# The MLP down-projection of a two-block transformer: seven block products in place of eight, in passes of pairs

## The chip, the cores and the metric

The kernel runs on one core of a Trainium2 chip. The metric is the device time of one execution in microseconds; the numbers shown are medians of the runs.

## The reference

A sequence of 1,024 tokens of width 1,024 (float32) goes through two layers and then an attention block. In each layer x = x + g1 * mixer(modulate(rmsnorm(x))) and then x = x + g2 * mlp(modulate(rmsnorm(x))). The mixer of layer 0 is a pooling over windows, that of layer 1 a spatial gating unit; the shifts, scales and gates come from six vectors a layer, silu(c) @ ada_w + ada_b. The part that is changed is

```python
def sq_relu_mlp(h, w1, w2):
    return jnp.square(jax.nn.relu(h @ w1)) @ w2
```

with w1 of 1,024 x 4,096 and w2 of 4,096 x 1,024.

## The kernel before

Activations stand transposed, features on the 128 partitions and tokens along the free dimension in two halves of 512. A float32 product is made of three matmuls in a reduced float32 form: each operand is split into hi (ScalarE copies and so rounds it) and lo (VectorE subtracts hi from it), and `product` issues Whi.Xhi, Whi.Xlo and Wlo.Xhi (lines 2341 to 2343, a helper for most stages). X, of 8 rows (tiles of 128 features) by two halves, is resident except in the MLP, where its place is lent and it is reloaded from x_saved.

The hidden layer has 32 tiles of 128 features, in 16 pairs. `mlp` (line 599) drives all engines through one list of steps. The up-projection computes its first two pairs plainly (first_up, first_tile) and the other 14 in `fast`: each pair is a product of 2 x 2 blocks, done with 7 block products over sums of blocks (T1 to T4 on the token side, S1 to S4 on the weight side; the order is in PRODUCTS), each of 12 matmuls. VectorE joins the products, ScalarE takes relu and square, then hi; VectorE makes lo (`hidden_lo`), and SP stores hi and lo together in DRAM, 512 KB a tile and half.

The down-projection (`down`) goes over 16 chunks of one pair each. A chunk's weights, 1 MB, come through a ring of four stage slots and are split whole (L1223 on ScalarE, L1696 on VectorE); its hidden tiles come back already split into MB, issued on ScalarE's queue two chunks ahead. For each of 16 output tiles there are 2 products (6 matmuls) into one of four banks, and VectorE adds the bank, times the gate, to X (L2035). In layer 0 sixteen quarters of the ada vectors (1,2) to (1,5), 1 MB each with two VectorE instructions (L1671, L1674, L1677), are read between the chunks. In the last chunk the next norm has begun: `completed` squares each row, POOL adds the squares (L1077), TensorE sums them over partitions (L2373), and the first half's normed tiles are written before the second half's products end.

After layer 0 comes the value stage of the gating unit: `values` multiplies 8 token tiles by weights in four units (L2656 to L2658), 24 matmuls a tile and half, interleaved in SP's queue with the gather of the attention's position bias (L1018); `spatial` loads ws and bs and masks ws on POOL; `gates` follows. After layer 1 come the head projections.

```python
for c in range(CHUNKS):
    for a in late.get(c, ()):
        fetch(4)
        ada_ahead(*a)
    fetch(4)
    do["fetched_split"](T, None)
    used(w=1)
    do["down"](T, gate, l, c, then if c == CHUNKS - 1 else None)
```

## Time and profile before

| | |
|---|---|
| median of 3 runs | 2523.53 us (2520.54 to 2524.2) |
| span of the profiled execution, first to last instruction | 2519.7 us |
| its own time | not given apart from the runs; 3.8 us lie between its span and the median |
| TensorE, VectorE, ScalarE, POOL busy | 2460.9, 1636.2, 986.4, 273.9 us |
| down-projection, layers 0 and 1 | about 438 to 804 and 1419 to 1780 us |

Matmuls overlap, so their busy times add up to more than passes; their pace is read from one start to the next. The page also gives the granted clock of TensorE, as a share of 2.4 GHz; its two levels are 1.0 and 0.5, and values between them are means over a stretch.

### The profile page before, as it was taken

The numbers are of one execution on the slowest core, as the hardware profiler recorded it, in microseconds if no ns is written. First come the engines' busy times: TensorE is split into PE (matmuls) and PEld (weight loads), VectorE is DVE, ScalarE is ACT, GpSimd is POOL, SyncE is SP. The second block draws the span as 40 slices with busy tenths as digits, with TensorE's granted clock in tenths as the row PEclk, the third lists the DMA queues.
The fourth block names the chain that finished last, engine by engine and source line by source line (L and its number), as shares of the span: only waits on it lengthen the run. The fifth ranks groups of instructions, "written<-read, shape, count | busy, mean of one in ns | idle before, by whom it ended". The sixth has DMA issues, their size and how long they took to land.

```text
span 2519.7 us, 32563 instructions
## 1 busy us (share of the span) xinstructions
PE 2460.9 (98%) x11616; PEld 2003.8 (80%) x11616; DVE 1636.2 (65%) x2554; ACT 986.4 (39%) x1622; POOL 273.9 (11%) x279
## 2 busy tenths in 40 slices
PE   7999999999999999999999999999999999999998
PEld 2588888788887888888888888888888897886677
DVE  7798776777776343458667666666651226998873
ACT  2366565000003232237666300001431226887851
POOL 0200000000002000100000000000010002557731
PEclk9899999999999999999999999999999999999999
DMA  8726666855543610333544844431334472346621
GB/s 306 267 76 234 226 223 260 317 190 178 200 167 108 178 46 1 134 117 142 192 159 167 317 176 140 145 134 51 126 121 146 143 184 71 85 111 160 168 68 67
DMA packets 219076, 396.89 MB, mean 158 GB/s; under 512 B 59440, under 2 KB 136368, under 8 KB 218928
## 3 DMA queue, kind: packets, MB, share of 16 engines
q1 hardware_dynamic: 203696, 336.21, 40.3%
q10 hardware_dynamic: 15232, 58.72, 6.4%
q8 instruction: 91, 1.49, 0.2%
q14 instruction: 57, 0.47, 0.1%
HBM read 285.83 MB, written 115.08 MB: 159 GB/s over the span
## 4 chain that ended last, share of the span: by engine, by line
PE 87%; DVE 5%; issue 3%; POOL 3%; ACT 1%; DMA 0%; DVEq 0%; POOLq 0%; ACTq 0%; SPq 0%
PE banks L2341 23%; PE banks L2343 23%; PE banks L2342 23%; PE banks L2432 2%; PE banks L2871 2%; PE banks L2889 2%; PE banks L2656 1%; PE banks L2657 1%; PE banks L2658 1%; POOL probs L1139 1%; PE banks L2495 1%; DVE neg_max L2278 1%; PE banks L2373 1%; PE banks L2858 1%; PE banks L2859 1%
## 5 line engine op out<-in xcount | busy, mean ns | idle before, releaser
L2035 DVE SCALAR_TENSOR_TENSOR X<-banks,mod,X 128x512 f32<-128x512 f32 x512 | 380.8, 749 | 227.2 <-PE banks L2343 227.0
L2341 PE MATMUL banks<-Hhi,Whi 128*128 128x512 f32 x1248 | 493.3, 395 | 6.6 <-DVE Hlo L1861 2.9
L2342 PE MATMUL banks<-Hlo,Whi 128*128 128x512 f32 x1248 | 486.8, 390 | 0.0
L2343 PE MATMUL banks<-Hhi,Wlo 128*128 128x512 f32 x1248 | 486.8, 390 | 0.0
L2341 PE MATMUL banks<-MB,Whi 128*128 128x512 f32 x1024 | 401.5, 392 | 2.2 <-DVE X L2035 2.2
L2343 PE MATMUL banks<-MB,Wlo 128*128 128x512 f32 x1024 | 399.5, 390 | 0.0
L2342 PE MATMUL banks<-MB,Whi 128*128 128x512 f32 x1024 | 399.4, 390 | 0.0
L1223 ACT ACTIVATE Whi<-stage 128x2048 fp32r<-128x2048 f32 x59 | 112.9, 1913 | 615.3 <-PE banks L2343 577.2
L2341 PEld LDWEIGHTS banks<-Hhi,Whi 128*128 128x128 f32 x1248 | 235.1, 188 | 59.6 <-issue 8.3
L2342 PEld LDWEIGHTS banks<-Hlo,Whi 128*128 128x128 f32 x1248 | 235.1, 188 | 50.4 <-issue 2.4
L2343 PEld LDWEIGHTS banks<-Hhi,Wlo 128*128 128x128 f32 x1248 | 234.9, 188 | 49.4
L2341 PEld LDWEIGHTS banks<-MB,Whi 128*128 128x128 f32 x1024 | 192.9, 188 | 42.5 <-issue 3.0
L2343 PEld LDWEIGHTS banks<-MB,Wlo 128*128 128x128 f32 x1024 | 192.8, 188 | 40.4
L2342 PEld LDWEIGHTS banks<-MB,Whi 128*128 128x128 f32 x1024 | 192.9, 188 | 39.2
L1696 DVE TENSOR_TENSOR Wlo<-stage,Whi 128x1024 fp32r<-128x1024 f32 (+1 forms) x93 | 145.2, 1562 | 89.6 <-ACT Whi L1223 88.1
L1139 POOL TENSOR_SCALAR probs<-probs,rden 128x1024 f32<-128x1024 f32 (+2 forms) x128 | 118.3, 924 | 337.3 <-DVE rden L2284 327.6
L2289 DVE TENSOR_TENSOR PTl<-banks,PTh 128x512 fp32r<-128x512 f32 (+2 forms) x256 | 135.2, 566 | 6.6 <-ACT PTh L1609 5.5
L2871 PEld LDWEIGHTS banks<-const,probs 128*128 128x128 f32 x800 | 88.6, 140 | 56.8 <-DVE PTl L2289 22.6
L2341 PE MATMUL banks<-T,Whi 128*128 128x512 f32 x336 | 131.1, 390 | 0.0
L2871 PE MATMUL banks<-const,probs 128*128 128x128 f32 x800 | 116.5, 279 | 14.7 <-POOL probs L1139 9.2
L1609 ACT ACTIVATE PTh<-banks 128x512 fp32r<-128x512 f32 (+2 forms) x256 | 119.5, 504 | 29.1 <-PE banks L2871 26.2
L2343 PE MATMUL banks<-T,Wlo 128*128 128x512 f32 x336 | 130.8, 389 | 0.0
(247 smaller groups left out, 3773.2 us busy)
## 6 DMA issues: line engine op xcount, KB each, us to landing
stage<-w SPq DMA_DIRECT2D x64, 1024.0 KB, 6.1
hidden<-slot SPq DMA_DIRECT2D x112, 512.0 KB, 3.0
MB<-hidden ACTq DMA_DIRECT2D x56, 1024.0 KB, 5.6
stage<-ada_w SPq DMA_DIRECT2D x48, 1024.0 KB, 6.5
x_saved<-X SPq DMA_DIRECT2D x32, 512.0 KB, 3.1
stage<-w_in SPq DMA_DIRECT2D x13, 1024.0 KB, 6.2
X<-x_saved SPq DMA_DIRECT2D x24, 512.0 KB, 7.2
MB<-hidden SPq DMA_DIRECT2D x8, 1024.0 KB, 10.1
```

The costliest lines, as they stand in the source:

```text
L1139: nc.gpsimd.tensor_scalar(out=row, in0=row, scalar1=rden[:, u % 4:u % 4 + 1], scalar2=1.0, op0=ALU.mult, op1=ALU.mult).then_inc(probs_scal ...
L1223: nc.scalar.activation(Whi[:, T.n["w"] % 2, :], stage[:, s, :], ACT.Copy).then_inc(w_hi, 1)
L1609: nc.scalar.activation(probs_t(PTh, u, kind, first, m), TP[:, g, 0:m * P] .rearrange("p (k q) -> p k q", q=P), ACT.Copy).then_inc(th_done, 1)
L1696: ins = nc.vector.tensor_tensor(Wlo[:, w % 2, at], stage[:, u % STAGES, at], Whi[:, w % 2, at].bitcast(F32), ALU.subtract)
L2035: nc.vector.scalar_tensor_tensor(out=X[:, k, half(hf)], in0=Dn[:, i % D_BANKS, :], scalar=gate[:, k:k + 1], in1=X[:, k, half(hf)], op0=ALU ...
L2289: nc.vector.tensor_tensor(probs_t(PTl, u, kind, first, m), TP[:, g, 0:m * P].rearrange("p (k q) -> p k q", q=P), probs_t(PTh, u, kind, fir ...
L2341: nc.tensor.matmul(out_bank, whi, xhi, start=start, stop=False, skip_group_check=onto)
L2342: nc.tensor.matmul(out_bank, whi, xlo, start=False, stop=False, skip_group_check=onto)
L2343: return nc.tensor.matmul(out_bank, wlo, xhi, start=False, stop=stop, skip_group_check=onto)
L2432: ins = nc.tensor.matmul(row_bank(cc, h), c_act[:, 2 * q + k:2 * q + k + 1], stage[:, u % STAGES, k * D + h * H:k * D + (h + 1) * H], star ...
L2871: ins = nc.tensor.transpose(TP[:, g, k * P:(k + 1) * P], PE_[:, u % 2, a:a + P], con("ident"))
L2889: ins = nc.tensor.matmul(OB[:, g % 2, :], VT[:, e, k, :], x[:, g % 2, k, :], start=k == tiles[0] and x is PTh, stop=k == tiles[-1] and x i ...
```

## The change

The down-projection is done with 7 block products too. Its output has four groups (`o`) of two rows; the 16 pairs are summed in 18 passes (PASSES: group, first pair, pair behind the last), each over 2, 3 or 4 pairs, and at most 4 pairs' right operands (7 a pair, hi and lo) are on chip at a time. A pass has 7 products of 3 matmuls a pair in the banks A, B, C and D; after a product VectorE evicts a bank (D1, A1, B, C1, A2, C2, D2), partly to X and partly to a sum U of the group that is added to three blocks in the group's last pass.

The right operands (B11, B21, B22 and the sums T1 to T4) are stored raw, 256 KB each, and not split: the sums are made by VectorE in the fast units, by POOL for the last one. They come back through 8 tile buffers in the stage ring and are split in the passes by ScalarE and VectorE, each once a layer, in the steps that `right_steps` gives. The left operands of pass t+1 are summed by POOL (S1 to S4) and split by ScalarE and VectorE during pass t. Squares of finished groups are made in the following pass, and the norm begins after the last pass ("blocks"). The ada vectors (1,2), (1,3) and (1,4) are read in the value stage, and (1,5) in layer 1's fast units. The `rotation` load, semaphores and buffer places follow.

```diff
+OUTS = 4
+PASSES = ((0, 0, 2), (1, 0, 3), (2, 0, 4), (3, 0, 4), (0, 2, 6), (1, 3, 7), (2, 4, 8), (3, 4, 8), (0, 6, 10),
+          (1, 7, 11), (2, 8, 12), (3, 8, 12), (0, 10, 14), (1, 11, 14), (2, 12, 16), (0, 14, 16), (1, 14, 16),
+          (3, 12, 16))
...
+def first_needed(p):
+    return min(t for t in range(NPASS) if PASSES[t][1] <= p < PASSES[t][2])
+def made_during(p):
+    return -1 if p < 2 else p - 2 if p < 4 else max(t for t in range(NPASS) if PASSES[t][1] <= p - 4 < PASSES[t][2])
...
+def right_steps(t):
+    pairs = [p for p in range(CHUNKS) if made_during(p) == t]
+    steps = [[] for _ in range(len(SIDES) + 1)]
+    for n, p in enumerate(pairs):
+        for q in range(len(SIDES)):
+            steps[min(q + 2 * n, len(SIDES))].append((p, q))
+    return steps
+def raw_loads():
+    place = {}
+    for t in range(-1, NPASS):
+        for steps in right_steps(t):
+            for p, q in steps:
+                place[7 * p + q] = t
+    return [[n for n in range(RAW + 6, 7 * CHUNKS) if max(place[n - RAW], 0) == t] for t in range(NPASS)]
+def evictions(t):
+    o = PASSES[t][0]
+    names = ["D1"] + ([] if t == FIRST_PASS[o] else ["A1"]) + ["B"]
+    return names + (["U21", "U12", "U22"] if t == LAST_PASS[o] else []) + ["C1", "A2", "C2", "D2"]
...
-                stream.append(src_in(w1[l], p + 3) if p < PAIRS - 1 else src_w2(l, 0))
-            for c in range(CHUNKS - 1):
-                stream += [src_ada(*a) for a in late.get(c, ())] + [src_w2(l, c + 1)]
-            stream.append(after)
+                if p < PAIRS - 1:
+                    stream.append(src_in(w1[l], p + 3))
             fetched, consumed = 0, 0
...
+            for t in range(NPASS):
+                do["passes"](T, gate, l, t, base, then)
+                if t == NPASS - 2:
+                    do["fetch"](T, after, 0, 7 * (NPASS * l + NPASS - 1))
+            T.add(e=NPASS, u=1, w=1)
+            T.n["uc"], T.n["un"] = T.n["un"], T.n["u"]
...
-            for c in range(CHUNKS):
-                for a in late.get(c, ()):
-                    fetch(4)
-                    ada_ahead(*a)
-                fetch(4)
-                do["fetched_split"](T, None)
-                used(w=1)
-                T.n["uc"], T.n["un"] = T.n["un"], T.n["u"]
-                do["down"](T, gate, l, c, then if c == CHUNKS - 1 else None)
-                T.add(c=1, d=16)
-                if c in late and late[c][-1][2] == 3:
-                    mods(*late[c][-1][:2])
...
         do["values"](T, 0, range(1))
         T.add(a=1)
+        for q in range(4):
+            ada(1, 2, q)
         split(src_values(1, 0))
         do["values"](T, 0, range(1, 8))
         T.add(a=7)
+        for q in range(4):
+            ada(1, 3, q)
         split(src_values(1, 1))
         do["values"](T, 1, range(5))
         T.add(a=5)
+        for q in range(4):
+            ada(1, 4, q)
         split(src_in(sgu_in, 0))
         do["values"](T, 1, range(5, 8))
         T.add(a=3, c=4)
...
+            def load_raw(T, l, n):
+                p, q = n // len(SIDES), n % len(SIDES)
+                if n < 4:
+                    sync.wait_ge(unit_done, T("u", -1))
+                elif n < RAW:
+                    sync.wait_ge(unit_done, T("u"))
+                else:
+                    p0, q0 = (n - RAW) // len(SIDES), (n - RAW) % len(SIDES)
+                    sync.wait_ge(right_lo, split_by(l, p0, q0))
+                side_stored(l, p, q)
+                sync.dma_start(raw_tile(T, n), hidden[p, q]).then_inc(raw_in[n % RAW], 16)
...
+            def passes(T, gate, l, t, base, then):
+                g = PAIRS * (l + 1) - 1
+                if t + 2 < NPASS:
+                    load_pass(T, l, t + 2)
+                if t == 0:
+                    sync.wait_ge(m_square, 4 * g + 1)
+                    sync.wait_ge(joined, 5 * g + 3)
+                    reload_row(3)
+                    for n in range(4):
+                        store_sum(PAIRS - 1, g, n)
+                    sync.wait_ge(m_square, 4 * g + 2)
+                    sync.wait_ge(joined, 5 * g + 5)
+                    reload_row(6)
+                    for k, b, name in ((4, "22", "T2"), (5, "11", "T1"), (7, "21", "T4")):
+                        sync.wait_ge(b_stored[b], 16 * (g + 1))
+                        sync.wait_ge(t_stored[name], 16 * (g + 1))
+                        reload_row(k)
+                for n in LOADS[t]:
+                    load_raw(T, l, n)
...
+            def pass_sums(T, l, t, names):
+                n = NPASS * l + t
+                for name in names:
+                    if name == "S1":
+                        pool.wait_ge(pass_in[t % 2], 16 * (NPASS // 2 * l + t // 2 + 1))
+                        if t == 0:
+                            pool.wait_ge(unit_done, T("u"))
+                        else:
+                            pool.wait_ge(ps_lo, 7 * n)
+                        out, a, b, op = pass_columns(t, S_sum[:]), pass_block(T, t, 1, 0), pass_block(T, t, 1, 1), ALU.add
+                    elif name == "S3":
+                        pool.wait_ge(ps_sums, 4 * n + 1)
+                        out, a, b, op = pass_block(T, t, 1, 0), pass_block(T, t, 0, 0), pass_block(T, t, 1, 0), ALU.subtract
+                    elif name == "S2":
+                        pool.wait_ge(ps_lo, 7 * n + 1)
+                        out, a, b, op = pass_columns(t, S_sum[:]), pass_columns(t, S_sum[:]), pass_block(T, t, 0, 0), ALU.subtract
+                    else:
+                        pool.wait_ge(ps_sums, 4 * n + 3)
+                        pool.wait_ge(ps_lo, 7 * n + 3)
+                        out, a, b, op = pass_columns(t, S_sum[:]), pass_block(T, t, 0, 1), pass_columns(t, S_sum[:]), ALU.subtract
+                    nc.gpsimd.tensor_tensor(out, a, b, op).then_inc(ps_sums, 1)
+            def hidden_sum(g, n):
+                name = SUMS_MADE[n]
+                out, a, b = sum_tiles(name)
+                pool.wait_ge(m_square, 4 * g + 4)
+                reach(pool, t_stored[name], 16 * g)
+                if n > 0:
+                    pool.wait_ge(t_sums, 4 * g + n)
+                nc.gpsimd.tensor_tensor(out, a, b, ALU.subtract).then_inc(t_sums, 1)
+            def passes(T, gate, l, t, base, then):
+                g = PAIRS * (l + 1) - 1
+                if t + 1 < NPASS:
+                    pass_sums(T, l, t + 1, ("S1", "S3", "S2"))
+                    for n in range(4 if t == 0 else 0):
+                        hidden_sum(g, n)
+                    pass_sums(T, l, t + 1, ("S4",))
+                if then == 2:
+                    for n, o in enumerate(OUT_ORDER):
+                        if t == min(LAST_PASS[o] + 1, NPASS - 1):
+                            for i in range(4 * n, 4 * n + 4):
+                                add_squares(T, "blocks", i)
...
+            def passes(T, gate, l, t, base, then):
+                o = PASSES[t][0]
+                steps = right_steps(t)
+                if t == 0:
+                    for p, q in right_steps(-1)[len(SIDES)]:
+                        right_hi(T, l, p, q)
+                for q in range(len(SIDES)):
+                    act.wait_ge(pass_done, 7 * (NPASS * l + t) + q + 1)
+                    if q == 1 and t == FIRST_PASS[o]:
+                        nc.scalar.activation(UT[:, o, :], fast_bank("A", t), ACT.Copy).then_inc(u_begun, 1)
+                    if t + 1 < NPASS:
+                        pass_hi(T, l, t + 1, base, q)
+                    for p, r in steps[q]:
+                        right_hi(T, l, p, r)
+                    for n, done in enumerate(OUT_ORDER[:-1]):
+                        if t == LAST_PASS[done] + 1 and q < 4:
+                            block_square(T, l, 4 * n + q, then)
...
+            def evict(l, t, gate, name):
+                o, at = PASSES[t][0], {"D1": ("D", 0, "22"), "A1": ("A", 1, None), "B": ("B", 2, None), "C1": ("C", 3, "22"),
+                                       "A2": ("A", 4, "11"), "C2": ("C", 5, "21"), "D2": ("D", 6, "12")}
+                u = UT[:, o, :]
+                if name in at:
+                    bank, q, b = at[name]
+                    dve.wait_ge(pass_done, 7 * (NPASS * l + t) + q + 1)
+                    source = fast_bank(bank, t)
+                else:
+                    source, b = u, name[1:]
+                if b is None:
+                    if t == FIRST_PASS[o]:
+                        dve.wait_ge(u_begun, OUTS * l + t + 1)
+                    else:
+                        dve.wait_ge(evicted, evicted_by(l, t, name) - 1)
+                    nc.vector.tensor_tensor(u, source, u, ALU.add).then_inc(evicted, 1)
+                    return
+                x, k = out_tile(t, b)
+                if t == FIRST_PASS[o] and b in ("22", "11"):
+                    dve.wait_ge(x_filled[k], 16 * (l + 2))
+                dve.wait_ge(evicted, evicted_by(l, t, name) - 1)
+                nc.vector.scalar_tensor_tensor(out=x, in0=source, scalar=gate[:, k:k + 1], in1=x, op0=ALU.mult,
+                                               op1=ALU.add).then_inc(evicted, 1)
+            def passes(T, gate, l, t, base, then):
+                o = PASSES[t][0]
+                steps, last = right_steps(t), t == LAST_PASS[o]
+                if t == 0:
+                    for p, q in right_steps(-1)[len(SIDES)]:
+                        right_lower(T, l, p, q)
+                if t == NPASS - 3:
+                    make_gain(T, then)
+                for q, name in enumerate(("D1", "A1", "B", "C1", "A2", "C2", "D2")):
+                    if name in evictions(t):
+                        evict(l, t, gate, name)
+                    if q == 2 and last:
+                        for more in ("U21", "U12", "U22"):
+                            evict(l, t, gate, more)
+                    if t + 1 < NPASS:
+                        pass_lo(T, l, t + 1, base, q)
+                    for p, r in steps[q]:
+                        right_lower(T, l, p, r)
...
+            def passes(T, gate, l, t, base, then):
+                n = NPASS * l + t
+                o, p0, p1 = PASSES[t]
+                if t == 0:
+                    pe.wait_ge(joined, 5 * T.n["f"])
+                    pe.wait_ge(m_relu, 4 * T.n["f"] - 2)
+                for q, (_, side, bank, first) in enumerate(PRODUCTS):
+                    pe.wait_ge(ps_lo, 7 * n + q + 1)
+                    for p in range(p0, p1):
+                        if first_needed(p) == t:
+                            pe.wait_ge(right_lo, split_by(l, p, q))
+                    if t > 0:
+                        if q == 0 and t > 1:
+                            pe.wait_ge(evicted, evicted_by(l, t - 2, "D2"))
+                        if q == 1:
+                            pe.wait_ge(evicted, evicted_by(l, t - 1, "A2"))
+                        if q == 2:
+                            pe.wait_ge(evicted, evicted_by(l, t - 1, "B"))
+                        if q == 3:
+                            pe.wait_ge(evicted, evicted_by(l, t - 1, "C2"))
+                    if q == 4:
+                        if t == FIRST_PASS[o]:
+                            pe.wait_ge(u_begun, OUTS * l + t + 1)
+                        else:
+                            pe.wait_ge(evicted, evicted_by(l, t, "A1"))
+                    if q == 5:
+                        pe.wait_ge(evicted, evicted_by(l, t, "C1"))
+                    if q == 6:
+                        pe.wait_ge(evicted, evicted_by(l, t, "D1"))
+                    hi, lo = operand_at(base, q)
+                    for p in range(p0, p1):
+                        at = slice((p - p0) * P, (p - p0 + 1) * P)
+                        ins = product(fast_bank(bank, t), (hi[:, at], lo[:, at]), right_side(side, p % KH2),
+                                      first and p == p0, p == p1 - 1, not first)
+                    ins.then_inc(pass_done, 1)
...
```

## Rows read from the trace of the kernel before

**Rows 1.** the page, part 1: busy time, share of the span, instructions
```profile
PE 2460.9 (98%) x11616; PEld 2003.8 (80%) x11616; DVE 1636.2 (65%) x2554; ACT 986.4 (39%) x1622; POOL 273.9 (11%) x279
```
**Rows 2.** the page, part 5: the down-projection's additions and products, busy | idle before
```profile
L2035 DVE SCALAR_TENSOR_TENSOR X<-banks,mod,X 128x512 f32<-128x512 f32 x512 | 380.8, 749 | 227.2 <-PE banks L2343 227.0
...
L2341 PE MATMUL banks<-MB,Whi 128*128 128x512 f32 x1024 | 401.5, 392 | 2.2 <-DVE X L2035 2.2
```
**Rows 3.** timeline of PE, 759 to 773 us: first and last of 57 matmuls
```profile
759.62 0.39 PE L2341 MATMUL banks<-MB,Whi 128*128 128x512 f32 x1
...
772.32 0.39 PE L2343 MATMUL banks<-MB,Wlo 128*128 128x512 f32 x1
```
**Rows 4.** windows: PE, PEld, DVE, ACT, POOL busy; clock; DMA share, GB/s
```profile
550.00:600.00 50.00, 50.00 (x230) 41.66 (x229) 37.38 (x47) 5.75 (x3) 0.00 (x0) 1.00 0.56 190
850.00:900.00 50.00, 50.00 (x220) 40.89 (x218) 12.06 (x14) 10.60 (x14) 0.00 (x0) 1.00 0.32 90
```
**Rows 5.** lines by form, 200 to 400 us (the fast products)
```profile
L1932 DVE TENSOR_TENSOR Wlo<-stage,Whi 128x512 fp32r<-128x512 f32 x42 | 28.8, 686 | 6.6 <-ACT Whi L1389 6.6
...
L1389 ACT ACTIVATE Whi<-stage 128x512 fp32r<-128x512 f32 x42 | 26.1, 621 | 16.5 <-PE banks L2343 16.4
```
**Rows 6.** lines by form, DVE, 700 to 925 us
```profile
L1696 DVE TENSOR_TENSOR Wlo<-stage,Whi 128x2048 fp32r<-128x2048 f32 x5 | 11.5, 2291 | 3.9 <-ACT Whi L1223 3.9
...
L1677 DVE SCALAR_TENSOR_TENSOR acc<-stage,c_act,acc 128x1024 f32<-128x1024 f32 x3 | 3.9, 1285 | 0.1
```
**Rows 7.** timeline, 779 to 792 us: VectorE beside POOL
```profile
780.89 8.69 POOL L1077 TENSOR_TENSOR SUM<-SUM,SQ 128x512 f32<-128x512 f32 x5 [0.80 <-ACT SQ L1239]
...
783.42 2.17 DVE L1696 TENSOR_TENSOR Wlo<-stage,Whi 128x1024 fp32r<-128x1024 f32 x1
...
785.51 2.07 DVE L2035 SCALAR_TENSOR_TENSOR X<-banks,mod,X 128x512 f32<-128x512 f32 x3
```
**Rows 8.** timeline, 1813 to 1830 us: a POOL product and a VectorE sum
```profile
1819.73 1.29 POOL L1125 TENSOR_TENSOR COS<-QN,rope 128x512 f32<-128x512 f32 x1 [3.13 <-DVE QN L2217]
1820.29 1.28 DVE L2227 TENSOR_TENSOR RF<-COS,RT 128x512 f32<-128x512 f32 x1
```
**Rows 9.** lines by form, POOL, whole span
```profile
L1077 POOL TENSOR_TENSOR SUM<-SUM,SQ 128x512 f32<-128x512 f32 x38 | 52.2, 1377 | 87.7 <-ACT SQ L1239 86.0
...
L1132 POOL TENSOR_TENSOR ws<-ws,const 128x128 f32<-128x128 f32 x8 | 3.4, 461 | 37.2 <-DMA bs<-sgu_bs 37.2
```
**Rows 10.** the page, part 6: DMA issues, KB each, us to landing
```profile
stage<-w SPq DMA_DIRECT2D x64, 1024.0 KB, 6.1
hidden<-slot SPq DMA_DIRECT2D x112, 512.0 KB, 3.0
...
X<-x_saved SPq DMA_DIRECT2D x24, 512.0 KB, 7.2
```
**Rows 11.** timeline of PE, layer 0's last chunk to the first value matmul
```profile
774.25 0.49 PE L2341 MATMUL banks<-MB,Whi 128*128 128x512 f32 x1
...
810.64 0.77 PE L2656 MATMUL banks<-Whi,Hhi 128*128 128x512 f32 x1
```
**Rows 12.** timeline of PE, layer 1's end of the down-projection
```profile
1780.16 2.78 PE L2373 MATMUL banks<-g_sq,SQ 128*128 128x2 f32 x24
```
**Rows 13.** windows, PE alone: busy, granted clock, DMA share, GB/s
```profile
792.00:795.00 3.00, 3.00 (x13) 0.50 0.31 128
795.00:798.00 3.00, 3.00 (x9) 0.50 0.12 46
...
810.00:813.00 3.00, 3.00 (x12) 0.63 0.94 231
```
**Rows 14.** timeline of SP's queue, 800 to 925 us
```profile
817.76 11.14 SPq L1018 DMA_DIRECT2D position_bias<-rpb  x8
...
832.66 4.71 SPq L922 DMA_DIRECT2D bs<-sgu_bs  x1
```
**Rows 15.** timeline of POOL, 825 to 870 us
```profile
842.78 3.39 POOL L1132 TENSOR_TENSOR ws<-ws,const 128x128 f32<-128x128 f32 x8 [37.24 <-DMA bs<-sgu_bs]
```

More of the change, by code:

```diff
@@ L903, in fast @@
[L903 to L917 removed]
+                        store_sum(p - 1, g - 1, n)
```

576 lines of the change are left out of this document (325 added, 251 removed).

## The prediction

> **What bounds the kernel now.** I read the page first: TensorE is busy for 98% of the span [rows 1]. The costliest groups then say what it does: in the down-projection it waited 2.2 us in all for its 3,072 products, while VectorE's additions to X sat idle for 227 us waiting for products [rows 2]. So in this stage TensorE's issue rate sets the end. The "mean ns" of a matmul is no price, for matmuls overlap: in the timeline 56 start-to-start steps take 12.70 us, 0.2268 us each [rows 3]. Stretches of 50 us show the cover: VectorE 37.4 busy in the down stage, 12.1 in the value stage, TensorE 50.0 in both [rows 4].
>
> **What is removed.** A layer has 16 pairs of hidden tiles and 4 outputs of two rows each; 8 block products of 3 matmuls are 16 x 4 x 8 x 3 = 1,536 matmuls, 7 are 1,344. Two layers save 384 x 0.2268 = 87.1 us. Only new waits of TensorE can take it back, so each handover is walked below.
>
> **VectorE in a pass.** Three end-to-end additions take 2.07 us [rows 7]: one occupies 0.66 us, 0.09 less than its busy 0.75; the same allowance makes a subtraction in SBUF (0.687 busy [rows 5]) 0.60. A full pass (84 matmuls, 19.05 us) has seven evictions (5 x 0.66 + 2 x 0.60 = 4.5), seven left operands (4.2) and 0, 7 or 14 right ones (0, 4.2, 8.4): 8.7, 12.9 or 17.1 us. ScalarE has at most 21 copies of 0.62 [rows 5] = 13.1. POOL has four sums; one of 128x512 takes 1.29 us alone [rows 8] and 1.377 in the mean, 0.461 at 128 columns [rows 9]. They cost VectorE too: with POOL at work from 1819.73 for 1.29 us, a subtraction issued at 1820.29 took 1.28, that is 0.73 until POOL ended and then 0.55 of its own [rows 8]; the 128x1024 one took 2.17 [rows 7] where half of a 128x2048 one is 1.15 [rows 6]. Additions from a bank kept their pace beside the same POOL work [rows 7]. So I charge 2.5 to 4.5 us a pass (an eviction hides half of a blocked sum, a second subtraction nothing; bounds 0 and 5.2). The heaviest passes, 3, 7 and 11, come to 21.6 against 19.05. TensorE stands first at product 5, which needs eviction C1; in pass 4 I find C1 done 0.2 us before that, and the next pass (16.1) repays the lag. Price 0; if nothing is repaid, 3 x 2.6 a layer, 16 us. The Trainium skill, SBUF — State Buffer, Who interferes with whom, says that a VectorE instruction with two SBUF inputs and a GpSimd instruction that reads SBUF lock each other out whole; by that rule and by the row it is the same 5.2 us at most.
>
> **Start of the passes, the largest new wait.** In pass 0 SP's queue is: weights, row 3, the four right sums of the last unit, rows 6, 4, 5, 7, and only then the raw tiles from number 14 on. Tile 14 is pair 2, product 0. ScalarE wants it in step 0 of pass 0, ahead of the copy that begins U, for which product 4 waits. The sums are POOL's now, behind S1, S3 and S2 of pass 1. From the end of the last fast product: the last join and product 0's start at 2 (VectorE enters some 1.2 us late, with 12 right operands and 7 left ones in that unit); first left operand of pass 1 at 8, S2 9, four sums 4 x 1.3, 14.2; the store of T4 lands 3.0 later [rows 10], and row 7 waits for it, 17.3; tile 14 goes out at 17.7 behind 2 MB of rows, whose landing takes 7.2 [rows 10], so about 23; U at 24.5, product 4 until 25.8, C1 near 28. Products 5 and 6 end at 31 where an unhindered pass ends at 9.5. Pass 1 (14.3 us of products, some 17 of VectorE) then waits about 1, against lag already counted. I take 22 a layer, 44, less the 2.2 of before [rows 2]: +42. Low end, stores and rows landing in 2.6 to 3 and no queue: 12 a layer, +22. High end 27, +52.
>
> **End of the passes.** Passes 15 and 16 have 2 pairs (9.5 us of products), yet all evictions plus U21, U12 and U22 (3 x 0.66, in SBUF). In 15, C1 comes 8.2 after the start, product 5 could start at 6.8: 1.4. In 16 the operands of a 4-pair pass are split and S1, S3, S2 of it lie between: 3.4; in layer 0 POOL also adds squares, and ScalarE's squares wait for them: 5.3. Together 4.8 + 6.7, +12 (4 to 20).
>
> **Norms.** They no longer begin inside the last chunk. Layer 0 before: 774.25 to the first value matmul at 810.64 is 36.4 us [rows 11] for 96 matmuls (21.8): 14.6 lost. After: eviction, square, statistics, deviation, spread, first scaled and split tile, some 7.2, and 1.6 in the second half where VectorE's 1.3 a tile lags. -6. Layer 1 before: only 2.6 us of statistics stand between [rows 12]; after about 8, because both deviations stand ahead of the first tile: +7 with its statistics. Together +1 (-5 to +10).
>
> **Value stage, where 12 ada quarters now stand.** A quarter costs VectorE 2 x 1.28 [rows 6], 10 us for four, and a 1 MB load of 6.1 us [rows 10] in a ring of four. Before, SP was far ahead. Now the load of the unit behind four quarters waits for the first of them, and VectorE reaches that only after the statistics of all eight tokens. For unit (1,1), from the end of the first half: quarter 0 done at 5, load landed at 14 (the quarters' own loads go out behind eight bias DMAs, 11.1 us of SP [rows 14], and share the wires), ScalarE 1.9, VectorE 2.3 [rows 6]: 18.2; TensorE wants it after 4 tokens, 48 matmuls, 10.9: 7 to 9 us. Then ws and bs: behind the unit that waits for the first quarter of (1,4). bs issues for 4.7 us [rows 14] and its mask took 3.4 [rows 15]; they were there 50 us early, now the mask ends about 9 after the last value product. Together +17 (8 to 28). Layer 1's four quarters in the fast units cost 2.6 each in units with 3 us to spare: 0.
>
> **Clock.** After short stalls and small matmuls the granted clock was 0.50 at 792 to 795, and 0.63 at the restart at 810 [rows 13]; a restart costs 1 to 3 us of matmuls. Five new idle stretches of 5 us or more, some of whose restarts are bound by VectorE anyway: +6 (0 to 14).
>
> **Sum.** Against the profiled span, 2519.7: -87.1 + 42 + 12 + 1 + 17 + 6 = -9, 2510.6. The median, 2523.5, is 3.8 above that span (the profiled execution's own time isn't shown apart), so 2514.5, and I say 2515. About 0.2%, 5 us, is what a measurement here can tell from no change.
>
> **The rivals.**
> 1. *Fewer waits.* SP gets through its stores and the ring refills early: start +22, values +8, end +4, clock 0: 2523.5 - 87 + 35 = 2472; half way, 2485, is its typical result. For it: my walk takes each landing at its loaded value. Against: the order of the queue is fixed. Chance 0.26.
> 2. *The port.* POOL's sums block VectorE in every step, heavy passes aren't repaid: +16, and the start and end grow by 8: 2539, slower. It decides once C1 of pass 4 is over 2 us later than I find. For it: rows 8. Against: over passes 3 to 6 VectorE has 51.6 us and POOL 20.6 against 76.2. Chance 0.17.
> 3. *Late raw tiles.* A tile is loaded only once the one eight before is split. In passes 3, 7 and 11 I find 6.3 us between; a landing of 3.0 fits, one of 7.2 as for X's rows does not, and each heavy pass pays about 5: 6 x 5 = 30, 2545. Decides from a landing of 6.3. Chance 0.13.
> 4. *The clock.* It falls not at long gaps alone but in passes with many short waits, as around 792 to 798, where 6 us at half the clock lose 3 [rows 13]; ten such places give 2547. The Trainium skill, TensorE: Matmul & The Clock Gate, names such cycling through PSUM banks in "A second HAM failure mode"; the rows of before show it once a layer end at most. Chance 0.08.
> My forecast has 0.36, of which 0.21 is faster, 0.10 the same, 0.05 slower.
>
> **Chances and range.** Faster 0.21 + 0.26 = 0.47; same 0.10 + 0.03 from rivals 2 and 4 at their edges = 0.13; slower 0.40. The range, 2480 to 2550, reaches to typical rival 1 and past rivals 3 and 4; the likeliest case alone spans 2500 to 2530.
>
> **What would show it.** 2,688 matmuls in the passes at 0.227; TensorE idle some 15 us between products 3 and 5 of pass 0, released through ScalarE's U copy by the load of raw tile 14; full passes at 19.1 us; 1 to 5 us ahead of product 5 in passes 15 and 16; two waits of 7 to 9 us in the value stage, on Wlo and on the ws mask; 7 to 8 us at each norm. The forecast is wrong if tile 14 is there early, if VectorE subtractions beside POOL take 0.69, or if middle passes take over 20 us.

## The result, and the profile after

The changed kernel takes 2550.9 us (median of 4 runs, 2549.3 to 2556.6) against 2522.9 of the kernel before: a ratio of 1.0115, 95% interval 1.0100 to 1.0129. It is slower by 1.15%; I had forecast 2515, in a range of 2480 to 2550. The profiled span is 2547.4 us against 2519.7, 27.7 more.

The page first: its span, engines and costliest waits.

```profile
span 2547.4 us, 32726 instructions
PE 2411.7 (95%) x11232; PEld 1955.2 (77%) x11232; DVE 1694.2 (67%) x2714; ACT 1115.1 (44%) x1946; POOL 489.2 (19%) x431
...
L2665 PE MATMUL banks<-Hhi,Whi 128*128 128x512 f32 x1760 | 701.9, 399 | 66.7 <-ACT UT L1600 38.2
...
L2339 DVE SCALAR_TENSOR_TENSOR X<-banks,mod,X 128x512 f32<-128x512 f32 x180 | 134.5, 747 | 89.6 <-PE banks L2667 89.2
```

The 384 matmuls are gone, and TensorE is busy for 49 us less than in [rows 1], in a span that is 28 us longer. One wait stands out where [rows 2] had next to none: 38.2 us behind ScalarE's copy that begins U. The windows that answer to [rows 4] show a middle pass, and then the value stage:

```profile
550.00:600.00 50.00, 50.00 (x223) 41.40 (x222) 35.16 (x50) 18.25 (x32) 17.27 (x12) 1.00 0.38 122
850.00:900.00 50.00, 37.33 (x146) 29.87 (x147) 20.12 (x27) 11.48 (x14) 5.30 (x8) 0.87 0.46 150
```

In the middle passes TensorE is still full at clock 1.00, with VectorE at 35 of 50 us. In the window of the value stage it has lost 12.7 us to waits, and the granted clock is 0.87 in the mean. TensorE's timeline gives the waits themselves (start, duration, idle before and what ended it):

```profile
181.34 0.77 PE L2665 MATMUL banks<-Hhi,Whi 128*128 128x512 f32 x1 [3.05 <-DVE U L2239]
...
443.16 0.50 PE L2665 MATMUL banks<-T,Whi 128*128 128x512 f32 x1 [1.39 <-DVE full L2239]
...
467.92 0.76 PE L2665 MATMUL banks<-Hhi,Whi 128*128 128x512 f32 x1 [19.03 <-ACT UT L1600]
...
758.78 0.76 PE L2665 MATMUL banks<-Hhi,Whi 128*128 128x512 f32 x1 [3.50 <-DVE X L2339]
...
791.98 0.77 PE L2991 MATMUL banks<-Whi,Hhi 128*128 128x512 f32 x1
...
853.91 0.79 PE L2991 MATMUL banks<-Whi,Hhi 128*128 128x512 f32 x1 [5.75 <-DVE Wlo L1970]
898.49 3.78 PE L2955 MATMUL banks<-ws,ones 128*128 128x512 f32 x4 [8.76 <-POOL ws L1377]
...
1798.41 3.69 PE L2699 MATMUL banks<-g_sq,W_raw 128*128 128x2 f32 x32
1808.01 0.76 PE L2665 MATMUL banks<-Hhi,Whi 128*128 128x512 f32 x1 [3.65 <-DVE Hlo L2135]
```

These are the places that the prediction had walked: the handover, product 4 of pass 0, passes 15 and 16, the norms (791.98 answers to 810.64 in [rows 11], 1798.41 to 1780.16 in [rows 12]), Wlo and the mask in the value stage. The clock does not stay up in every pass. It is at 0.50 around the stall of pass 0 in both layers, and again for 10 us in pass 16 of layer 0, where two waits stand close together:

```profile
756.00:760.00 4.00, 1.22 (x3) 1.06 (x4) 2.59 (x4) 0.00 (x0) 1.89 (x2) 0.50 0.97 398
760.00:764.00 4.00, 4.00 (x10) 3.07 (x10) 2.04 (x3) 2.82 (x5) 3.71 (x4) 0.50 0.03 11
```

The windows of the gates stage, which comes next, show something that it had not walked (columns: TensorE busy and matmuls, granted clock, DMA share, GB/s):

```profile
920.00:925.00 5.00, 5.00 (x23) 1.00 0.75 238
925.00:930.00 5.00, 4.22 (x31) 0.83 0.02 5
930.00:935.00 5.00, 5.00 (x25) 0.50 0.00 0
935.00:940.00 5.00, 5.00 (x19) 0.50 0.00 0
940.00:945.00 5.00, 5.00 (x19) 0.80 0.00 0
```

TensorE counts as busy and does half the work: the clock is at the lower of its two levels (1.2 of 2.4 GHz) for some 14 us. The same happens at 966 and 1000, for 10 us each. The lines of this stage, 895 to 1045 us, tell what is new there:

```profile
L2666 PE MATMUL banks<-WSlo,Vhi 128*128 128x128 f32 x64 | 22.9, 358 | 0.0
L2688 PE MATMUL banks<-ones,X 128*128 128x1 f32 x48 | 5.8, 250 | 2.3 <-ACT X L1737 2.3
```

L2688 is the ada sums of vectors (1,2), (1,3) and (1,4): eight matmuls of 128x1 for each (two records a matmul), which the change moved from the down stage to stand between `gates(j)` and `mix(j)`. Mix's 128x128 matmuls behind them mean 358 ns; in the kernel before they were 275:

```profile
L2342 PE MATMUL banks<-WSlo,Vhi 128*128 128x128 f32 x64 | 17.6, 275 | 0.0
```

The ledger by stages, after minus before, from the start of each stage's first matmul, adds up to the 27.7 us:

| stage | before, us | after, us | difference |
|---|---|---|---|
| layer 0, first up to pass 0 (down) | 321.8 | 327.0 | +5.2 |
| layer 0, down with its norm | 372.7 | 348.8 | -23.9 |
| value stage, to the first gates matmul | 89.2 | 109.3 | +20.1 |
| gates and mix, to the first wait of the resplit | 112.5 | 138.5 | +26.0 |
| resplit, projection, norm | 94.3 | 94.3 | 0.0 |
| layer 1, first up to pass 0 | 312.5 | 320.9 | +8.4 |
| layer 1, down with its norm | 363.6 | 352.9 | -10.7 |
| the rest, with the opening | 853.0 | 855.6 | +2.6 |

Four sums of ada vectors stood in layer 0's down-projection before, 1.70 us each from their start to the next product's. So 6.8 of the 23.9 us that this stage gained are work that now stands elsewhere: three sums in the gates stage, and that of (1,5) in the fast units of layer 1, 1.7 of its +8.4.

### The profile page after: what moved, and what is told of

It is laid out like the page before. It is cut to its first block, busy times and chain, and to the rows that moved or that the text cites. A ratio compares the mean times of both kernels' runs of the same rounds, so it can differ in the third digit from the quotient of the medians.

```text
span 2547.4 us, 32726 instructions
## 1 busy us (share of the span) xinstructions
PE 2411.7 (95%) x11232; PEld 1955.2 (77%) x11232; DVE 1694.2 (67%) x2714; ACT 1115.1 (44%) x1946; POOL 489.2 (19%) x431
## 4 chain that ended last, share of the span: by engine, by line
PE 80%; issue 7%; DVE 5%; POOL 4%; ACT 2%; DMA 1%; SPq 0%; POOLq 0%; DVEq 0%; ACTq 0%
PE banks L2665 22%; PE banks L2667 21%; PE banks L2666 21%; PE banks L3206 2%; PE banks L3224 2%; PE banks L2743 2%; POOL probs L1384 1%; PE banks L3193 1%; PE banks L3194 1%; PE banks L2807 1%; DMA stage<-hidden 1%; PE banks L2699 1%; POOL X L1416 1%; PE banks L2688 1%; PE banks L3176 1%
## 5 line engine op out<-in xcount | busy, mean ns | idle before, releaser
L2665 PE MATMUL banks<-Hhi,Whi 128*128 128x512 f32 x1760 | 701.9, 399 | 66.7 <-ACT UT L1600 38.2
L2666 PE MATMUL banks<-Hlo,Whi 128*128 128x512 f32 x1760 | 692.4, 393 | 0.0
L2667 PE MATMUL banks<-Hhi,Wlo 128*128 128x512 f32 x1760 | 691.9, 393 | 0.0
L2665 PEld LDWEIGHTS banks<-Hhi,Whi 128*128 128x128 f32 x1760 | 335.3, 191 | 147.2 <-issue 66.3
L2666 PEld LDWEIGHTS banks<-Hlo,Whi 128*128 128x128 f32 x1760 | 335.5, 191 | 70.9 <-issue 2.7
L2665 PE MATMUL banks<-T,Whi 128*128 128x512 f32 x720 | 281.6, 391 | 2.9 <-DVE full L2239 2.9
L2667 PE MATMUL banks<-T,Wlo 128*128 128x512 f32 x720 | 280.2, 389 | 0.0
L2666 PE MATMUL banks<-T,Whi 128*128 128x512 f32 x720 | 280.2, 389 | 0.0
L2339 DVE SCALAR_TENSOR_TENSOR X<-banks,mod,X 128x512 f32<-128x512 f32 x180 | 134.5, 747 | 89.6 <-PE banks L2667 89.2
L2665 PEld LDWEIGHTS banks<-T,Whi 128*128 128x128 f32 x720 | 135.3, 188 | 31.5 <-DVE full L2239 3.8
L2667 PEld LDWEIGHTS banks<-T,Wlo 128*128 128x128 f32 x720 | 135.2, 188 | 28.4
L2666 PEld LDWEIGHTS banks<-T,Whi 128*128 128x128 f32 x720 | 135.4, 188 | 27.9
```

What stands on the lines that cost most here:

```text
L2339: nc.vector.scalar_tensor_tensor(out=x, in0=source, scalar=gate[:, k:k + 1], in1=x, op0=ALU.mult, op1=ALU.add).then_inc(evicted, 1)
L2665: nc.tensor.matmul(out_bank, whi, xhi, start=start, stop=False, skip_group_check=onto)
L2666: nc.tensor.matmul(out_bank, whi, xlo, start=False, stop=False, skip_group_check=onto)
L2667: return nc.tensor.matmul(out_bank, wlo, xhi, start=False, stop=stop, skip_group_check=onto)
```

## The experiments

All are edits of the changed kernel but one. "Ratio" is to the kernel before, with its 95% interval; value and gates are the two stages of the ledger, from each profiled run.

| run | median us | ratio | value, us | gates, us |
|---|---|---|---|---|
| before | 2522.9 | 1 | 89.2 | 112.5 |
| after | 2550.9 | 1.0115 (1.0100 to 1.0129) | 109.3 | 138.5 |
| e1_swap | 2536.3 | 1.0063 (1.0046 to 1.0080) | 107.7 | 122.0 |
| e1_early | 2544.7 | 1.0092 (1.0075 to 1.0109) | 124.8 | 114.2 |
| e2_raws | 2528.3 | 1.0030 (1.0020 to 1.0040) | | |
| e3_order | 2534.2 | 1.0054 (1.0036 to 1.0073) | 90.4 | 139.8 |
| e4_sums | 2532.5 | 1.0034 (1.0021 to 1.0047) | | |
| e5_all | 2495.3 | 0.9888 (0.9870 to 0.9906) | 90.6 | 123.7 |
| e6_nowait | 2547.1 | 1.0100 (1.0081 to 1.0118) | 109.9 | 133.9 |
| e7_noada | 2507.2 | 0.9942 (0.9924 to 0.9959) | 90.2 | 112.5 |
| e8_best | 2499.0 | 0.9904 (0.9887 to 0.9921) | 89.7 | 122.2 |
| e9_wide | 2539.9 | 1.0067 (1.0048 to 1.0087) | 107.9 | 128.4 |
| e10_before_sums | 2541.1 | 1.0074 (1.0056 to 1.0091) | 89.1 | 129.2 |
| e11_late | 2485.5 | 0.9863 (0.9845 to 0.9880) | 89.7 | 122.2 |

**The theory and its rivals.** Theory: the passes cost what I had worked out, and the loss beyond it is the moved ada sums, through the clock. Rivals: the stage is longer through waits; or the loss comes from the passes after all.

**e1_swap**, the sums behind mix, so that full-size matmuls follow them:

```
-            if j < 3:
-                mods(1, 2 + j)
             mix(j)
+            if j < 3:
+                mods(1, 2 + j)
```


> The three moved ada sums (1,2), (1,3), (1,4) are issued after mix(j) instead of before it, so that full-size gates matmuls follow them and not the 128x128 ones of mix. Theory A (the sums' wait and their 8 matmuls of 128x1, followed by the small matmuls of mix, let the granted clock fall to 0.50 for 10 to 12 us three times, some 15 to 18 us of the 26.0 us that the gates stage lost): the clock stays at or near 1.00 in the gates stage and the time falls by 12 to 20 us to 2531 to 2539. Rival B (the sums bring the clock down wherever they stand): the fall moves into the gates matmuls and the time stays within 4 us of 2551. Rival C (the stage is longer for other waits than the clock): the clock comes back, the stage keeps 15 or more of its 26 us.

14.6 us less by the medians; the gates stage is 16.5 shorter. Same instructions, other place. In the first of the three places the clock stayed up where it had fallen (columns from here on: TensorE, weight loads, VectorE, ScalarE and POOL busy, clock, DMA share, GB/s):

```profile
925.00:930.00 5.00, 5.00 (x47) 5.00 (x47) 4.24 (x7) 0.24 (x2) 0.00 (x0) 1.00 0.01 4
930.00:935.00 5.00, 5.00 (x30) 4.34 (x30) 4.84 (x8) 3.98 (x5) 0.00 (x0) 1.00 0.00 0
...
960.00:965.00 5.00, 5.00 (x17) 4.00 (x18) 4.91 (x7) 2.91 (x3) 0.00 (x0) 0.66 0.00 0
```

Mix's 128x128 matmuls mean 275 ns again, as in the kernel before. The clock still dips at the other two places, for 3.4 us each, to 0.66 in the window shown. Theory A holds, with some of rival B. The kernel before bears it out: its layer 0 has seven such sums in front of 128x512 products, between 261 and 774 us, and the clock is 1.00 after each of them.

**e1_early**, the sums ahead of the value stage's last wait:

```
         T.add(a=3, c=4)
+        for cc in (2, 3, 4):
+            mods(1, cc)
         do["spatial"](T)
```


> The three moved ada sums are all taken out of the gates stage: they are issued before the row sums of the spatial weights, at 889 to 898 us, where TensorE waits 8.8 us for POOL's mask, into three separate banks. Theory A: the gates stage returns to within 3 us of its 111.6 us of before, and the time falls by 20 to 26 us to 2525 to 2531; the value stage grows by 0 to 4 us. Rival B (the clock falls in mix for another cause than the sums): the gates stage keeps 10 us or more over 111.6 and the clock still falls there. Rival C (the gain is given back in the value stage, because the row sums now wait for the sums): the value stage grows by more than 5 us.

The gates stage returns to 114.2, as theory A says, with the clock at 1.00 from 924 us on, 3 us after its start. Yet 15.5 of the 24.4 us are given back in the value stage, rival C, by a step that I had overlooked: SP loads `ws` only when all modulations counted so far are done (`mod_done`), and now these three are among them, so POOL's mask comes later. TensorE waits 5.6 us ahead of the sums and 9.4 behind them, where it waited 8.8 once, and the clock is 0.50 from 896 to 924 us.

**e6_nowait**, the sums in their place without their wait for ScalarE:

```
-                reach(pe, a_free, T("a"))
+                if not (l == 1 and 1 < cc < 5):
+                    reach(pe, a_free, T("a"))
```


> The changed kernel with the moved sums where they are, ahead of mix, but without their wait for ScalarE's last activation of the gates (they write a bank that no activation reads), so the wait of 0.78 us and the gap of 1.16 us ahead of each go, or move behind the sums. Theory A1 (the 8 small matmuls and the small ones of mix alone lower the clock): the granted clock still falls to 0.50 after each of them, the time falls by 0 to 4 us. Theory A2 (the wait is needed for the fall): the clock stays near 1.00 and the time falls by 12 to 20 us, to 2531 to 2539.

A1. The gaps of 1.16 us are gone and the stage is 4.6 us shorter, while the clock falls as before, with TensorE never idle by the records:

```profile
925.00:930.00 5.00, 5.00 (x40) 4.81 (x38) 0.81 (x2) 0.60 (x1) 0.00 (x0) 0.93 0.36 126
930.00:935.00 5.00, 5.00 (x25) 5.00 (x25) 2.99 (x5) 0.00 (x0) 0.00 (x0) 0.50 0.00 0
935.00:940.00 5.00, 5.00 (x18) 4.33 (x18) 3.86 (x8) 3.09 (x5) 0.00 (x0) 0.55 0.00 0
```

**e10_before_sums**, the suspected cost alone, in the kernel before:

```
             def mix(T, j):
+                if j < 3:
+                    pe.wait_ge(bs_ready, KT)
+                    for n in range(KT):
+                        nc.tensor.matmul(B6[:, n:n + 1], ones[:], ones[:, 0:1], start=True, stop=True)
```


> The kernel before the change, with eight matmuls of 128x1 added ahead of mix's first wait for j = 0, 1 and 2 (their result is not read), and nothing else. Theory A (these small matmuls in front of mix's small ones are enough to lower the clock in this place): three stretches at 0.50, the time grows by 12 to 20 us over the kernel before, to 2534 to 2542. Rival B (it takes the later state of the changed kernel, its accumulations or waits on other engines): the time grows by the matmuls alone, 3 x 1.8 = 5 us, to 2524 to 2529.

0.74% slower than the kernel before, some 19 us, 16.7 of them in this stage: theory A's size. The added matmuls are busy for 5.5 us; the rest is the clock. It fell in two of the three places, not in all three as expected. These are the windows of TensorE alone, around the first fall and the place without one:

```profile
920.00:925.00 5.00, 5.00 (x36) 0.84 0.20 70
925.00:930.00 5.00, 5.00 (x25) 0.50 0.00 0
930.00:935.00 5.00, 5.00 (x18) 0.50 0.00 0
935.00:940.00 5.00, 5.00 (x19) 0.80 0.00 0
...
955.00:960.00 5.00, 5.00 (x41) 1.00 0.00 0
960.00:965.00 5.00, 5.00 (x39) 1.00 0.02 5
```

Twenty-four matmuls that cost 5.5 us by their durations thus cost about three times that, and nothing else of the change is needed for it.

**e9_wide**, 64 columns in place of one:

```
+                    for j in range(KT):
+                        ins = nc.tensor.matmul(B6[:, j * 64:(j + 1) * 64], ada_total(l, cc)[:, j * P:(j + 1) * P],
+                                               ones[:, 0:64], start=True, stop=True)
```


> The changed kernel with the moved sums where they are, ahead of mix, but each of their 24 matmuls made 64 columns wide in place of 1 (the result is read from every 64th column). Theory A (matmuls of one column leave TensorE nearly idle although the profile shows it busy, and this is what lowers the clock): with more columns the granted clock stays higher in the three stretches and the time falls by 5 to 20 us, to 2531 to 2546. Rival B (any pause of full-size matmuls before mix's matmuls of 128 columns lowers it, whatever the width of the sums): the clock falls to 0.50 as before, the time within 4 us of 2551 or some us above.

11 us less, 10 of them in the stage: wider matmuls that take no longer (5.9 us busy in place of 5.8). The clock stayed at 1.00 after the first and the third sums and fell after the second:

```profile
955.00:960.00 5.00, 4.58 (x33) 4.61 (x33) 0.79 (x2) 0.28 (x1) 0.00 (x0) 0.79 0.01 3
960.00:965.00 5.00, 5.00 (x25) 5.00 (x25) 2.78 (x5) 0.00 (x0) 0.00 (x0) 0.50 0.01 2
```

That is on theory A's side. With one column the clock fell in all 15 places of five profiled kernels (the changed one, e2_raws, e3_order, e4_sums, e6_nowait), and the ratio's interval here lies below that of the changed kernel. But e10_before_sums, with one column too, has two falls in three places, so how much of a single profile is chance stays open.

**e7_noada**, the three vectors left out:

```
-        for q in range(4):
-            ada(1, 2, q)
...
-            if j < 3:
-                mods(1, 2 + j)
```


> The three moved ada vectors (1,2), (1,3), (1,4) are left out: no loads, no accumulation, no sums; their part of the modulation is set to zero once at the start, so the output is not the reference's. Theory A (what the change lost outside the down passes is the move of these three vectors: 20.1 us in the value stage and 26.0 us in the gates stage): the time falls by 40 to 48 us to 2503 to 2511. Rival B (the value stage's wait for the mask is there without the vectors, since the mask's load stands behind the weights' loads on SP's queue and the shorter norm has moved it): 5 to 10 us of it stay, 2511 to 2520.

43.8 us less; both stages are back at 90.2 and 112.5, the one 1.0 us longer than in the kernel before, the other equal. So all that the two stages lost is these vectors' move. With everything else of the change in place the kernel is 0.58% faster than before, some 15 us. Part of that is work left out, which the kernel before still does: the three sums alone are 5.1 us of TensorE there. So the passes by themselves gain some 0.4% (an estimate from these two numbers).

**e3_order**, the value stage's order:

```
-        for q in range(4):
-            ada(1, 2, q)
         split(src_values(1, 0))
+        for q in range(4):
+            ada(1, 2, q)
         do["values"](T, 0, range(1, 8))
         T.add(a=7)
...
         split(src_values(1, 1))
+        do["ws_load"](T)
```


> In the value stage each split of value weights comes before the four ada quarters that the change put ahead of it, and the spatial weights and their bias are loaded right after the second split instead of after everything. Theory A (the 20.1 us that the stage lost are the wait of 6.1 us for the value weights behind the quarters at 847.8, the wait of 9.2 us for the mask at 889.3, and some 3 us of lower clock after them): both waits go and the time falls by 13 to 20 us to 2531 to 2538. Rival B (VectorE, or SP's eight issues for each position bias at 1.3 us each, sets these waits): at least one of the two waits stays over 3 us, gain 4 to 12 us.

Theory A: 16.7 us less. The value stage is 90.4, both waits are gone. The gates stage keeps its loss, so the two are separate.

**e2_raws**, raw tiles 14 to 20 first in SP's queue:

```
+                for n in LOADS[t] if t == 0 else ():
+                    if n < 3 * len(SIDES):
+                        load_raw(T, l, n)
                 if t + 2 < NPASS:
                     load_pass(T, l, t + 2)
```


> On SP's queue the seven raw right tiles of pair 2 are loaded at the start of pass 0, ahead of the weights of pass 2, the four stores of the last unit's sums and the five reloads of rows. Theory A (the stall of 19.4 us before product 4 of pass 0, in both layers, is the load of raw tile 14 queued behind those): the stall falls to 1 to 6 us, and the time falls by 2 x (12 to 17) = 24 to 34 us, to 2517 to 2527. Rival B (VectorE's splits or the transfers, which then crowd, bound passes 0 to 2): half of it returns as stalls in passes 1 and 2, gain 8 to 20 us. Rival C (the reloads of rows 4 to 7 or the stores, now later, are waited for): gain below 8 us, with waits for DMA X in passes 1 to 3.

22.6 us less, just short of theory A's 24. The long stall of layer 0 has become two shorter ones, of 2.3 and 5.9 us, ahead of products 4 and 5 (the expectations below call the latter product 6, counting from one). The second has VectorE in front of it, and VectorE's timeline of those us is this:

```profile
454.04 1.76 DVE L2268 TENSOR_TENSOR Hlo<-stage,Hhi 128x512 fp32r<-128x512 f32 x1
455.72 0.68 DVE L2337 TENSOR_TENSOR UT<-banks,UT 128x512 f32<-128x512 f32 x1
456.32 1.02 DVE L2260 TENSOR_TENSOR Wlo<-S_sum,Whi 128x384 fp32r<-128x384 f32 x1
457.26 1.74 DVE L2268 TENSOR_TENSOR T<-stage,T 128x512 fp32r<-128x512 f32 x1
458.93 0.74 DVE L2343 SCALAR_TENSOR_TENSOR X<-banks,mod,X 128x512 f32<-128x512 f32 x1
```

Subtractions in SBUF take 1.7 us beside POOL's sums and 0.68 without them; additions from a bank keep their pace. That is what [rows 7, 8] showed and rival 2 was about. Whether it costs time here, the next run asks. The Trainium skill, SBUF — State Buffer, Who interferes with whom, says that a VectorE instruction with two SBUF inputs contends with a GpSimd instruction that reads SBUF, and one with at most one SBUF input, outside some faster modes, does not. By that rule, the trace agrees: 1.76 and 1.74 us for the first kind, 0.68 and 0.74 for the second.

**e4_sums**, those four sums made by VectorE:

```
-                    for n in range(4 if t == 0 else 0):
-                        hidden_sum(g, n)
...
                         right_lower(T, l, p, q)
+                        if n == 1:
+                            for m in range(4):
+                                hidden_sum(PAIRS * (l + 1) - 1, m)
```


> The early raw loads of e2_raws, and the four sums of the last unit's hidden tiles made by VectorE between the raw tiles of pair 1 (446 to 450 us, where VectorE stood idle for 2.2 and 0.6 us) in place of POOL (453.7 to 460.1 us). Theory A (in e2_raws the stall of 6.1 us before product 6 of pass 0, in both layers, is the VectorE queue, whose subtractions took 1.49 to 1.76 us beside POOL's four sums in place of 0.68): the stall falls to 1 to 3 us, the rows of 1.49 to 1.76 us go, and the time falls by another 2 x (3 to 5) = 6 to 10 us against e2_raws, to 2518 to 2522. Rival B (VectorE's own count of instructions bounds this stretch, so four more of 0.68 us cost as much as they save): within 3 us of e2_raws at 2528. Rival C (the transfers bound it): within 3 us as well, with waits for DMA stage<-hidden.

A miss: the time is that of e2_raws within the intervals. The rows of 1.7 us are gone, but the sums ran at 451.1 to 454.4, in front of the splits and evictions that pass 0 waits for, and cost as much as they saved (rival B). They were not in the idle 2 us that I had aimed at.

**e5_all**, the four edits together:

> All together: early raw loads, last unit's sums on VectorE, the value stage's order of e3_order, the ada sums after mix as in e1_swap. If the causes are separate, the gains add: 22.6 (e2_raws) + 6 to 10 (e4_sums) + 16.7 (e3_order) + 14.6 (e1_swap) = 60 to 64 us from 2550.9, that is 2487 to 2491, faster than the kernel before by 1.2 to 1.4%. Rival (they overlap, a wait that is taken away uncovers another): 40 to 55 us, 2496 to 2511.

55.7 us less than the changed kernel, between the full sum and the rival's upper end; the shortfall of 4 to 8 us is about the gain that e4_sums had not shown. **e8_best** puts the sums into the idle time:

```
+                        if n == 0:
+                            for m in range(4):
+                                hidden_sum(PAIRS * (l + 1) - 1, m)
                         right_lower(T, l, p, q)
-                        if n == 1:
```


> As e5_all, but VectorE makes the last unit's four sums ahead of the last two raw tiles of pair 1, in its idle 2 us at 446.9 to 449.1, where e4_sums and e5_all had them at 451.1 to 454.4 us, in front of the eviction and the splits that pass 0 waits for. Theory A (VectorE's queue from 449 to 460 us is what products 4 and 6 of pass 0 wait for; the place of the sums cost what their cheaper rows saved): the stall of 6.3 to 6.6 us before product 6 falls to 2 to 4 us in both layers and the time falls by 4 to 8 us to 2487 to 2491. Rival B (the transfers of the raw tiles bound it): within 2 us of 2495.

Another miss, no difference to e5_all that the intervals show. The stall at product 5 did fall from 6.6 to 3.6 us in layer 0, but waits of 1.0 and 2.2 us came up in pass 1: between 440 and 520 us TensorE lost 11.5 us in e5_all and 11.7 here. This points to the sum of VectorE's work as what bounds passes 0 and 1, and not to one instruction's place.

**e11_late**, the first unit's sums behind the third join:

```
                 join(g, 2, m_full["22"][:], 0, "D", U1[:])
+                if p == 0:
+                    first_sums(T, l, 0, SUMS_MADE)
```


> As e8_best, but in the first fast unit of each layer VectorE makes the four sums of the first unit's hidden tiles (2 x 1.48 us, at 175.1 and 177.7 us in the changed kernel, 2.8 us in front of the join that TensorE waits for at 181) after the third join in place of before the first two. Theory A (the stall of 3.2 us in this unit, 1.1 us in the kernel before, is VectorE's queue lengthened by these sums): the stall falls to 0.5 to 1.5 us in both layers and the half clock of some 3 us behind it goes too, so the time falls by 3 to 7 us to 2492 to 2496 by the medians (2484 to 2487 by the profiled span). Rival B (the later sums are stored later and the fourth and fifth joins, which wait for those stores, hold up the next unit): a new stall of 2 us or more by 200 us, no gain.

Better than expected: 13.5 us by the medians, 11.1 by the spans. The stall of 3.2 us, at 182 us in e8_best, is down to 0.4 in both layers. In e8_best each stall had taken some half clock with it, 1 us or more in layer 0 and 2 or more in layer 1: layer 0 is 3.8 us shorter at the first value matmul, layer 1 another 5.5 at its last fast unit. This version is faster than the kernel before by 1.4%.

## Why the prediction was wrong, point by point

- **384 matmuls at 0.2268: right.** Full passes take 19.04 us each, with no stall, and rival 3's late raw tiles do not occur.
- **VectorE in a pass: the price of 0 is right, its working is not.** I had 21.6 us of VectorE in passes 3, 7 and 11, a deficit that the next pass repays. There is no deficit: VectorE is busy for 16.7 us at most in any full pass of layer 0. The block by POOL is there, but small. Of 155 subtractions in passes 2 to 12 only 21 took over 0.9 us, the longest 1.79, and together they added 0.6 to 1.7 us to each of passes 2 to 11, where I had charged 2.5 to 4.5. (What I called a subtraction in [rows 8] is an addition of two SBUF tiles.)

```profile
551.42 1.30 POOL L1322 TENSOR_TENSOR stage<-stage 128x512 f32<-128x512 f32 x1
...
552.12 1.14 DVE L2256 TENSOR_TENSOR Wlo<-S_sum,Whi 128x512 fp32r<-128x512 f32 x1 [0.41 <-ACT Whi L1582]
```

- **Start of the passes, +42: right, and by the walked mechanism.** Beyond their pace TensorE's products lost 19.2 and 1.5 us in pass 0 and 1.8 in pass 1 of layer 0, 19.3, 1.5 and 0.4 in layer 1: 43.7, less the 2.2 of before. The later handover, which the walk has too, adds 3.2: 44.7 in all. The chain that ended last has each link that I had listed (start, duration, what):

```profile
451.97 1.23 POOL slot L1332
453.36 1.27 POOL slot L1332
454.79 1.27 POOL slot L1332
456.21 1.27 POOL slot L1332
457.50 2.09 DMA hidden<-slot
460.07 6.57 DMA stage<-hidden
466.67 0.63 ACT T L1588
```

- **End of the passes, +12: right in sum, wrong in split.** 1.7, 2.3 and 3.9 us in layer 0, 0.8 and 1.3 in layer 1: 10.0; layer 1 has less than I gave it, and its two waits are for ScalarE's squares and not for eviction C1.
- **Norms, +1: right.** In layer 0 TensorE lost 8.6 us between the last product and the first value matmul, 6.0 less than before; in layer 1 9.6 us stand where 2.6 stood. That down and norm together came out at -23.9 and -10.7 us against -21.9 and -10.8 by my terms is in part luck: the first holds the 6.8 us of the four sums, which I had not counted, against some 5 us of half clock in passes 0 and 16.
- **Value stage, +17: right.** 5.8 and 8.8 us of waits, and most of the rest of the 20.1 is the lower clock behind them; e3_order shows both causes.
- **Layer 1's quarters in the fast units, and the fast stage as a whole, 0: too low by 13.6.** The quarters are not shown to be it. The first unit's sums of hidden tiles, 2 x 1.48 us of VectorE that I had not followed into this unit, gave a stall of 3.2 us where some 1.1 had been, in both layers, with a fall of the clock in layer 0 in this profile. e11_late takes off 11 us, more than these stalls had added. Of the rest 3.2 are the later joins ahead of pass 0 (my walk had them in the start), 1.7 the sum of (1,5), and 2.5 a wait for a join in layer 1's last fast unit, at 1447.8 us, that no run explains.
- **What failed: the move of the ada vectors was priced only by its loads and accumulations.** "Value stage, where 12 ada quarters now stand" ends the account of them there; the three sums that go with them stand nowhere in the sum, and the clock term of +6 was tied to long idle stretches. They cost 26.0 us in the gates stage: 2.8 in three waits, 5.8 in their own matmuls, and some 17 of half clock in mix and the first gates matmuls (e1_swap took away 16.5). e7_noada gives all of it back. With these 26 and the 13.6 of the fast stages the sum of -9 becomes +31; measured +27.7.
- **By cause, the term that was mis-sized is the clock: +6 forecast, some 34 measured.** This is an estimate: half of the time in which TensorE is recorded busy at a granted clock of 0.50, after minus before. Some 19 of it lie in the gates stage and 5 in the value stage; the other 10 are what passes 0 and 16, the first fast unit and layer 1's norm added, less 3 at layer 0's norm. TensorE's idle time grew by 77 us, and my terms for waits had 72 (42 + 12 + 1 + 17). So -87 + 77 + 34 = +24 against +27.7: the waits came out nearly right in sum, and what a lower clock costs, behind them and above all behind the sums, did not.
- **Rival 4** had the clock falling where short waits meet small work, at 2547, and the size is close (ten places at 3 us on top of 2515 would make 2545). That is in part luck: it looked for the falls in passes with many short waits. One such fall is there, in pass 16 of layer 0, for some 3 us; the middle passes stay at 1.00, and the largest loss is where small matmuls follow each other. **Rival 2** had the right mechanism. The longer subtractions are there in the middle passes too, without a wait of TensorE, and in pass 0 e4_sums and e8_best gained nothing by avoiding POOL's four sums. Rival 1's fewer waits is what e2_raws makes.

Two parts stay open: why the clock falls in some places and not in others of the same kind (two of three in e10_before_sums, one of three in e9_wide), and the exact share of column width in it.

## What to carry to other kernels

When work is moved, list every instruction that goes with it, down to the eight tiny matmuls at its end, and look at what stands behind them on TensorE: put them in front of full-size matmuls and not of small ones, since in front of mix they cost three times their duration. Where a new stage begins, order the one queue that feeds it by when each load is first needed; that alone was worth 23 us here (e2_raws). An edit that takes away one late instruction of an engine that has no spare time moves the wait and does not remove it.

## What the hardware showed that I had not expected

Eight matmuls of 128x1 (1.9 us by the records), followed by 48 of 128x128, brought the granted clock from 1.00 to 0.50 for 10 to 14 us while TensorE was recorded as busy without a gap (e6_nowait, e10_before_sums); without the eight the same 128x128 matmuls kept it at 1.00 (the kernel before, e7_noada). The 128x128 matmuls start every 0.213 us at 0.50, and every 0.112 us at 1.00 (e1_swap). Made 64 columns wide, the eight took no longer and the clock fell in one place of three. The Trainium skill, TensorE: Matmul & The Clock Gate, A second HAM failure mode, tells of a clock that swings when TensorE idles briefly between groups of matmuls; no such idling is needed here.
